# A hybrid diffusion layer on one core: a new order in the recurrence's turns, six heads' queries ahead of the experts, scores amid the second tile's rows, and twelve buffers for the last rows

## The reference, cut to what matters

```
# recurrent mixer, per channel block of 128 (16 of them), two directions d
u  = dwconv(x_l, conv_w, conv_b, left=2)
r  = sigmoid(u @ wa[d] + ba[d]);  i = sigmoid(u @ wx[d] + bx[d])
log_a = -8 * r * softplus(-lam[d]);  a = exp(log_a)
h  = scan(a, sqrt(1 - a*a) * (i * u))          # over time; latents start from the context's state
lru = (h_forward + h_backward) * gelu(g_l)
y  = sigmoid(gates) * (att @ w_o_attn), ... + lru @ w_o_lru + sc @ w_o_sc;  x = x + m2 * (y @ w_out)

# experts: 8 heads, 16 experts a head out of 128 x 128, per token
q = h @ w_q;  s1, s2 = q[0] @ k1, q[1] @ k2;  top 16 of each, top 16 of their sums -> idx, gate
act = gelu(sum_d u_table[idx] * h);  out = sum_k (gate * act)_k * v_table[idx_k]
```

## Time and profile before

| | |
|---|---|
| median of 3 runs | 3000.03 us (2997.91 to 3001.17) |
| profiled execution | 2998.28 us |
| span of its instructions | 2996.7 us |
| mean granted TensorE clock | 0.96 of full speed |
| TensorE / VectorE / ScalarE / POOL busy | 2616.7 / 1958.1 / 970.1 / 612.6 us |
| moved by DMA | 902.91 MB |

### The profile page before, as it was taken

One profiled execution on the slowest core, in us unless ns is written; L12 is line 12 of the kernel. 1 busy time (PEld: TensorE's weight loads), 2 busy tenths in 40 slices (PEclk: granted clock), 3 DMA queues, 4 the chain that ended last, 5 costly groups with the idle time before them and its releaser, 6 DMA issues.

```text
span 2996.7 us, 31604 instructions
## 1 busy us (share of the span) xinstructions
PE 2616.7 (87%) x11037; PEld 1788.6 (60%) x11037; DVE 1958.1 (65%) x2665; ACT 970.1 (32%) x1324; POOL 612.6 (20%) x580
## 2 busy tenths in 40 slices
PE   7999997999989999999999877869697877768777
PEld 3588775888767889998887734333343333323332
DVE  4689996444665878887555775656555655666656
ACT  5567774443454443333444211101011111111100
POOL 0000000000000000000000474334353434443333
PEclk9999998999999999999999998989899898989999
DMA  8733333542324978887565899999999999999998
GB/s 344 274 106 125 112 112 141 196 170 99 141 85 163 367 291 341 343 328 284 202 235 217 344 419 409 421 411 422 421 413 421 403 421 411 421 414 421 421 422 363
DMA packets 126513, 902.91 MB, mean 301 GB/s; under 512 B 14016, under 2 KB 15552, under 8 KB 17216
## 3 DMA queue, kind: packets, MB, share of 16 engines
q0 software_dynamic: 82944, 604.02, 48.9%
q1 hardware_dynamic: 38736, 278.94, 24.8%
q10 hardware_dynamic: 4720, 18.57, 1.6%
HBM read 899.33 MB, written 2.13 MB: 301 GB/s over the span
## 4 chain that ended last, share of the span: by engine, by line
PE 41%; DMA 32%; DVE 13%; issue 10%; ACT 3%; POOL 1%; DVEq 0%; POOLq 0%; ACTq 0%; SPq 0%
DMA u<-in_peer_u,idx 28%; PE ps L462 10%; PE ps L505 8%; PE ps L507 7%; PE ps L506 7%; PE ps L866 4%; DVE u L1882 2%; DVE wl L1295 2%; DMA v<-in_peer_v,idx 2%; DMA w<-in_stream 1%; PE ps L519 1%; ACT wh L962 1%; PE ps L477 1%; DVE ub L1431 1%; POOL v L1980 1%
## 5 line engine op out<-in xcount | busy, mean ns | idle before, releaser
L866 PE MATMUL ps<-v,dg 128*128 128x512 f32 x1920 | 877.0, 613 | 167.0 <-DMA v<-in_peer_v,idx 103.2
L1882 DVE SCALAR_TENSOR_TENSOR u<-u,hN 128x2048 f32<-128x2048 f32 x256 | 586.6, 2292 | 465.8 <-DMA u<-in_peer_u,idx 454.1
L1295 DVE TENSOR_TENSOR wl<-w,wh 128x1024 fp32r<-128x1024 f32 x432 | 524.6, 1222 | 389.7 <-ACT wh L962 389.3
L866 PEld LDWEIGHTS ps<-v,dg 128*128 128x128 f32 x1920 | 367.4, 196 | 672.4 <-issue 497.0
L962 ACT ACTIVATE wh<-w 128x1024 fp32r<-128x1024 f32 x432 | 453.5, 1058 | 590.0 <-PE ps L507 399.4
L1970 POOL DMA_INDIRECT u<-in_peer_u,idx x256 | 280.6, 1096 | 826.5 <-DVE u L1882 437.7
L462 PE MATMUL ps<-both,wh 128*128 128x256 f32 x2048 | 370.9, 284 | 0.3
L1243 ACT ACTIVATE dg<-con,wt 128x128 f32<-128x128 f32 x240 | 93.4, 400 | 841.0 <-PE ps L866 832.5
L1980 POOL DMA_INDIRECT v<-in_peer_v,idx x256 | 297.8, 1163 | 174.3 <-PE ps L866 87.1
L462 PEld LDWEIGHTS ps<-both,wh 128*128 128x128 f32 x2048 | 319.8, 192 | 4.8 <-issue 3.5
L1959 POOL DMA_DIRECT2D mr<-in_wmod x64 | 34.0, 532 | 1357.0 <-DVE br_lo L1688 946.5
(11 more groups left out here) (265 smaller groups left out, 2891.1 us busy)
## 6 DMA issues: line engine op xcount, KB each, us to landing
w<-in_stream SPq DMA_DIRECT2D x260, 1024.0 KB, 4.8
mr<-in_wmod POOLq DMA_DIRECT2D x64, 1024.0 KB, 6.9
wg<-in_gates ACTq DMA_DIRECT2D x8, 512.0 KB, 3.4
wx<-in_stream SPq DMA_DIRECT2D x4, 1024.0 KB, 8.0
u<-in_peer_u,idx POOLq DMA_INDIRECT x256
v<-in_peer_v,idx POOLq DMA_INDIRECT x256, 17.9
xs<-in_ctx ACTq DMA_DIRECT2D x1, 2048.0 KB, 8.0
xs<-in_x ACTq DMA_DIRECT2D x1, 2048.0 KB, 14.8
```

Source lines behind the costliest of these rows:

```text
L866: last = mm(ps[:, b, :], dg[:, k % 4, :], V[n % NV][:, b * 512:(b + 1) * 512], start=(k == 0), stop=(k == TOPK - 1))
L1295: tt(wl[p % SPLITS][:, :, :], W[s][:, q * PIECE:(q + 1) * PIECE, :], wh[p % SPLITS][:, :, :].bitcast(F32), ALU.subtract)\
L1882: stt(U[n % NU][:, :], U[n % NU][:, :], 1.0, hN[:, t, :], ALU.mult, ALU.mult, accum_out=dot[:, t, k:k + 1])\
```

## The change

- **Recurrence.** `rc` goes from VectorE to ScalarE (a Copy with scale and bias behind the square root). ScalarE's `gate_work` is cut in two (`gates`, `powers`); piece 11 is split between them, pieces 12 and 13 before the gelu's sigmoid. VectorE's order becomes `driven`, `gelu_inner`, `low` 11, `decays`, `low` 12, `drives`, `low` 13, `scans`, `low` 14, ..., with `low` 17 and 18 behind `scans(1)`.
- **Last turn.** TensorE does the eight `hx` pieces of OUT0's first turn there: four between the two gate products, four behind them; their splits and lows are put amid the turn's work. OUT0's first turn is taken out of its loop and begins with pieces 8 to 11 already split.
- **Queries.** Heads 4 and 5 are made before `experts(0, 0)` as well. Head 5's weights (2 MB) are loaded by ScalarE's queue at the beginning of `WO0` into the room of `acc`, ahead of that queue's load of `x2`; head 6's follow head 4's in `W`. Queries use banks 4 and 7 by turns. `acc` is no longer cleared in `WO0`: tile 0's first sum is a copy, and tile 1's half is cleared ahead of `dots(1, 0)`.
- **Scores.** `scores(h + 2)` stand behind the ninth row of `experts(h, 1)`.
- **Last rows.** The last 16 rows go into twelve buffers, first the four of U (each once its last dot product is done), then the eight of V, then the first four of V again.

```diff
+        WA = [sb(f"wa{s}", R_HX + 16384 + 8192 * NU + s * HB, [P, HK, CW]) for s in range(2)]
+        def query_bank(h):
+            return h if h < 4 else (4, 7)[h % 2]
+        def last_row_at(k):
+            if k < NU:
+                return U[k], (u_in[k], PH * (2 * TOPK // NU * 16) + 16)
+            i = k - NU
+            return V[i % NV], (v_in[i % NV], (PH - 1) * (2 * TOPK // NV * 16) + TOPK // NV * 16 + 16 * (i // NV + 1))
@@ SyncE @@
-            for h in range(4, PH):
+            for h, of in ((4, 0), (6, 4), (7, 6)):
                 for s in (0, 1):
-                    sp.wait_ge(piece_used, 2 * (WQ0 + 2 * (h - 1 if h > 4 else 0) + s + 1))
+                    sp.wait_ge(piece_used, 2 * (WQ0 + 2 * of + s + 1))
@@ TensorE, last turn of the recurrence, and OUT0 @@
                 gate_products(0)
+                pe.wait_ge(*AD.at(j, "pad1"))
                 if more:
-                    pe.wait_ge(*AD.at(j, "pad1"))
                     proj_both(LRU0, j, 8, 0)
+                else:
+                    wide(OUT0, 0, 16, 0, 0, hx, range(4))
                 gate_products(1)
+                if not more:
+                    wide(OUT0, 0, 16, 0, 0, hx, range(4, 8))
-            out_section(0, OUT0)
+            out_turn(0, OUT0, 0, gated=True)
+            with pe.Fori(1, NW) as j:
+                out_turn(0, OUT0, j)
@@ TensorE, experts @@
+                    last.then_inc(*PE_.inc(f"v{t}{k}"))
+                    if scored is not None and k == TOPK // 2:
+                        scores(scored)
             scores(1)
             route(3)
+            route(4)
+            route(5)
             for h in range(PH):
                 experts(h, 0)
-                if h + 4 < PH:
+                if 6 <= h + 4 < PH:
                     route(h + 4)
-                if h + 2 < PH:
-                    scores(h + 2)
                 if h + 1 < PH:
-                    experts(h, 1)
+                    experts(h, 1, h + 2 if h + 2 < PH else None)
@@ ScalarE @@
+                    act.wait_ge(*AL.at(j, f"e1_{b}"))
+                    fn(aa[:, :, :], aa[:, :, :], ACT.Copy, scale=0.5, bias=0.5).then_inc(*AL.inc(f"rc{b}"))
...
+                gates(0)
                 split(LRU0, j, 8, 11)
-                gate_work(0)
+                powers(0)
+                split(LRU0, j, 8, 12)
+                split(LRU0, j, 8, 13)
                 if more:
-                    for p in (12, 13, 14):
-                        split(LRU0, j, 8, p)
+                    gelu()
+                    split(LRU0, j, 8, 14)
                     pads(j + 1, j * 8 + (2 * LRU0 + 12))
                     split(LRU0, j, 8, 15)
-                gate_work(1)
+                else:
+                    split(LRU0, j, 8, 14)
+                    split(LRU0, j, 8, 15)
+                    gelu()
+                gates(1)
...
+                powers(1)
...
             act.wait_ge(piece_used, 2 * WO0)
+            for s in range(2):
+                act.dma_start(WA[s][:, :, :], a_stream[WQ0 + 10 + s].rearrange("p (k n) -> p k n", n=CW)).then_inc(wa_in[s], 16)
             act.dma_start(x2[:, :, :], a_x.rearrange("(t p) d -> p t d", p=P)).then_inc(x2_in, 16)
@@ VectorE, recurrence @@
-                low(LRU0, j, 8, 11)
                 driven(j, 0)
-                decays(j, 0)
-                gelu_inner(j)
-                drives(j, 0)
                 if more:
+                    gelu_inner(j)
+                    low(LRU0, j, 8, 11)
+                    decays(j, 0)
                     low(LRU0, j, 8, 12)
-                scans(j, 0)
-                if more:
+                    drives(j, 0)
                     low(LRU0, j, 8, 13)
-                lru_out(j, 0)
-                if more:
+                    scans(j, 0)
                     low(LRU0, j, 8, 14)
+                    lru_out(j, 0)
                     taps(j + 1, 0)
-                    low(LRU0, j, 8, 15)
+                else:
+                    low(LRU0, j, 8, 11)
+                    gelu_inner(j)
+                    decays(j, 0)
+                    drives(j, 0)
+                    scans(j, 0)
+                    low(LRU0, j, 8, 12)
+                    lru_out(j, 0)
+                    low(LRU0, j, 8, 13)
+                    low(LRU0, j, 8, 14)
                 driven(j, 1)
                 if more:
+                    low(LRU0, j, 8, 15)
                     taps(j + 1, 1)
                 decays(j, 1)
                 if more:
                     low(LRU0, j, 8, 16)
                 drives(j, 1)
+                if not more:
+                    low(LRU0, j, 8, 15)
+                scans(j, 1)
                 if more:
                     low(LRU0, j, 8, 17)
-                scans(j, 1)
-                low(LRU0, j, 8, 18 if more else 12)
+                    low(LRU0, j, 8, 18)
                 lru_out(j, 1)
@@ VectorE, WO0 and experts @@
-                    nc.vector.memset(acc[:, :, :], 0.0).then_inc(*VF.inc("acc0"))
+            nc.vector.memset(acc[:, 1, :], 0.0).then_inc(*VF.inc("acc0"))
-            dots(1, 0, route(1, 1, 1, False), (0, 0))
+            dots(1, 0, route(1, 1, 1, False), (0, 0, True))
@@ POOL, last tile @@
+            def last_rows(k):
+                row, (landed, _) = last_row_at(k)
+                if k < NU:
+                    pool.wait_ge(*VE.at(PH - 1, f"d1{TOPK - NU + k}"))
+                elif k < NU + NV:
+                    pool.wait_ge(*PE_.at(PH - 1, f"v0{TOPK - NV + k - NU}"))
+                else:
+                    pool.wait_ge(*last_used(k - NV))
```

More of the change, by code:

```diff
@@ L296, in build @@
         wx_in = [sem(f"wx_in{s}") for s in range(4)]
+        wa_in = [sem(f"wa_in{s}") for s in range(2)]
         u_in = [sem(f"u_in{i}") for i in range(NU)]
@@ L994, in lru_turn, with gates @@
             def lru_turn(j, more):
-                def gate_work(b):
+                def gates(b):
                     for d in (0, 1):
@@ L1060, in y_high @@
                         .then_inc(*AY.inc(f"h{b}"))
+            for p in range(8, 12):
+                split(OUT0, 0, 16, p)
             act.wait_ge(*VL.at(NCH - 1, "bl1"))
@@ L1064, in _ @@
             act.dma_start(brow[0:MT, :], a_bmod).then_inc(brow_in, 16)
-            out_section(0, OUT0)
+            out_turn(0, OUT0, 0, ahead=12)
+            with act.Fori(1, NW) as j:
+                out_turn(0, OUT0, j)
             act.wait_ge(crow_in, 16)
@@ L1562, in _ @@
             dve.wait_ge(*VL.at(NCH - 1, "bl1"))
-            with dve.Fori(0, NW) as j:
+            out_turn(0, OUT0, 0, ahead=8)
+            with dve.Fori(1, NW) as j:
                 out_turn(0, OUT0, j)
@@ L1898, in dots, with add @@
                 tt(wt[:, t, :], gw[:, :], gate[:, t, :], ALU.mult).then_inc(*VE.inc(f"w{t}"))
-            def add(h, t):
+            def add(h, t, first=False):
                 dve.wait_ge(*PE_.at(h, f"v{t}{TOPK - 1}"))
-                tt(acc[:, t, :], acc[:, t, :], ps[:, 0:4, :].rearrange("p b n -> p (b n)"), ALU.add).then_inc(*VA.inc(f"ac{t}"))
+                rows = ps[:, 0:4, :].rearrange("p b n -> p (b n)")
+                if first:
+                    nc.vector.tensor_copy(acc[:, t, :], rows).then_inc(*VA.inc(f"ac{t}"))
+                else:
+                    tt(acc[:, t, :], acc[:, t, :], rows, ALU.add).then_inc(*VA.inc(f"ac{t}"))
             def turn(h, odd, used=True):
@@ L1909, in last_row @@
             def last_row(k):
-                j, n = ON_DVE.index(k), TOPK + k
-                dve.wait_ge(v_in[n % NV], (PH - 1) * (2 * TOPK // NV * 16) + 16 * (n // NV + 1))
+                j = ON_DVE.index(k)
+                row, landed = last_row_at(k)
+                dve.wait_ge(*landed)
                 if j:
                     dve.wait_ge(last_dve, j)
-                stt(acc[:, 1, :], V[n % NV][:, :], wt[:, 1, k:k + 1], acc[:, 1, :], ALU.mult, ALU.add).then_inc(last_dve, 1)
+                stt(acc[:, 1, :], row[:, :], wt[:, 1, k:k + 1], acc[:, 1, :], ALU.mult, ALU.add).then_inc(last_dve, 1)
             for _ in route(0, 0, 0, False, True):
@@ L1947, in _ @@
                 dve.wait_ge(last_bank, b + 1)
[L1948 removed]
+                tt(hN[:, 0, cols_], ps[:, 4 + b, :], m5r[:, cols_], ALU.mult).then_inc(*VX.inc(f"x{b}"))
                 dve.wait_ge(*VX.at(0, f"x{b}"))
[L1950 removed]
+                tt(acc[:, 1, cols_], acc[:, 1, cols_], hN[:, 0, cols_], ALU.add).then_inc(*VX.inc(f"o{b}"))
         @block.gpsimd
@@ L1981, in rows_v @@
                                              in_offset=bass.IndirectOffsetOnAxis(ap=idx[:, odd, t, k:k + 1], axis=0)).then_inc(v_in[n % NV], 16)
+            def last_rows(k):
[4 more added lines that the diff above has]
+                    pool.wait_ge(*PE_.at(PH - 1, f"v0{TOPK - NV + k - NU}"))
+                else:
+                    pool.wait_ge(*last_used(k - NV))
+                apart(pool)
+                nc.gpsimd.indirect_dma_start(out=row[:, :], out_offset=None, in_=a_v,
```

(5 more changed lines are left out.)

95 lines of the change are left out of this document (44 added, 51 removed).

## The result

The changed kernel takes 2976.8 us (median of four runs, 2972.49 to 2978.17), the kernel before 2999.09 in the same series (2997.91 to 3001.17). The ratio is 0.9922, with an interval of 0.991 to 0.9934: 22.3 us faster. The forecast was 2967, 32.6 us faster; direction and range hold, and the point is 10 us off. The rest of the document asks where these 10 us are.

A forecast was written before the change was run, and what follows sets the result against it. It took TensorE's path as the bound before 1640 and the DMA queues behind 1670. 6.4 + 8.9 + 0.3 + 5.0 + 12.0 = 32.6 us brings the median of 3000.03 to 2967; range 2959 to 2981.

The forecast's parts named there:

- Loop: Recurrence's looped turns: VectorE loses `rc`, TensorE's 40.2 us becomes the bound; 6.4 us gained, bounds 2 and 7.7.
- The lag of 1.3 us: Recurrence: piece 11, split ahead of the tanh, delays the chain behind TensorE's gate products; 1.3 us subtracted once.
- Last turn: Recurrence's last turn: TensorE reaches `br` 10.3 us earlier, less 1.4 for the lower clock; 8.9 us, bounds 6 and 10.3.
- the third rival: Last turn's pieces: the clock stays at its lower level, 2.8 us more, 2970; chance 0.07.
- WO0 and beginning: WO0: no clearing of `acc`, 0.3 us; experts' beginning: 2 MB fewer on the saturated queue, 5.0 us, lower bound 4.
- Scores: Experts: with the scores moved, no buffer is late and six DMA dips go; 12.0 us, bounds 6 and 12.5.
- Last rows: Experts' end: twelve buffers can't bring the last row in earlier; nothing taken, between -2 and +1 us.
- The thin queue that I named: Last rows: row 3 waits for the last dot product with eight V rows behind it, which may thin the queue.
- The first two rivals: Recurrence's loop keeps its length, 2977, chance 0.14; experts' scores only move their wait to the ninth row, 2979, chance 0.12.
- a wait in the ninth row: Experts, sign that the forecast is wrong: a wait at 852 in a tile's ninth row.
- 17.0: Experts, first U gather to last dot product: forecast gain of 17.0 us, with 5.0 at the beginning and 12.0 for scores.

The follow-up runs named there:

- loop_alone: Kernel before with only the new order in the recurrence's seven looped turns and `rc` on ScalarE; 2993.37 us, ratio 0.9982.
- rc_back: Changed kernel with `rc` on VectorE again; 2980.76 us in one run.
- queries_alone: Kernel before with only the change's lines for the queries, `WA` and `acc`; 2993.67 us, ratio 0.998.
- scores_alone: Kernel before with only the scores moved behind the ninth row of the second tile; 2995.47 us, ratio 0.9984.
- straight kernels: Changed kernel with VectorE's loop over the expert heads written out, in most POOL's too, some with further edits; 2964.97 to 2972.81 us.
- old_last: Changed kernel with the last sixteen rows in V's eight buffers again; 2977.8 us, ratio 0.9928.
- recurrence_alone: Kernel before with all of the change up to OUT0 and nothing of the experts' part; 2984.23 us, ratio 0.9948.
- straight_both: Changed kernel with VectorE's and POOL's loops over the expert heads written out; 2964.97 us, ratio 0.9888.
- straight_scores_back: Changed kernel with both loops over the expert heads written out and the scores in their old place; 2972.81 us, ratio 0.9915.

## Why the prediction was right, and where it was not

- **Loop**, 6.4 forecast: 7.7 by the trace, 5.4 by loop_alone. The size was right and TensorE is the bound, as said. The cause was wrong: the term rested on the 1.37 us that VectorE loses with `rc`, and rc_back keeps `rc` on VectorE and has 6.9 of the 7.7 us. The lag of 1.3 us that I subtracted doesn't show in the sum of the turns.
- **Last turn**, 8.9 forecast. From the end of the scan (445.4) to `br` it takes 35.2 us, 35.7 were forecast; 1.7 us go to the lower clock behind it, 1.4 were taken off. 46.0 - 35.2 - 1.7 = 9.1. Of the third rival this holds: the lower level came back behind two of the three gaps, 3.67 and 2.54 us long, but only one stretch is on the path. The rule of the Trainium skill as the prediction drew it ("TensorE: Matmul & The Clock Gate", Part 1: the default state is throttled, so idle gaps put matmuls at 1.2 GHz) agrees with these two, and taken for every gap it does not agree with the pieces behind 2.01 us, which ran at a granted clock of 1.00.
- **WO0 and beginning**, 0.3 and 5.0. The 10.0 - 5.8 us by tile are 4.2, the lower bound of 4; queries_alone gave 3.0. The first U row came at 1657.0, for which 1655 was forecast; the last query ended near 1727.5, which is the forecast 1742 less the 14.2 us gained by then.
- **Scores**, 12.0: the step that was mis-sized. The mechanism was right: no `scores` among TensorE's waits, POOL's V rows wait for nobody, no wait in a ninth row, and the six dips are gone. The price was wrong. I had turned mean GB/s into time, 20 x (1 - 374/421) and so on. By landed rows the six tiles lose 7.7 us to the scores, and three tiles behind them take 2.6 longer once the scores are gone: 5.1 us net in the changed kernel, 2.3 to 4.7 with straight loops, 1.7 alone. All of these are below my lower bound of 6, though the ratio of scores_alone, 4.8, has an interval that reaches 7.5.
- **What the sum did not have**: VectorE's loop returns. The stall of 5.81 us stood in the trace before, and I had not looked at it. In the changed kernel the two tiles with returns take 3.2 us more than before. scores_alone has 2.9 of these without the second stall, rc_back, without it as well, only 0.3. So what a return costs is clear from the straight kernels in sum alone; why it costs more in the changed kernel than before stays open.
- **Last rows**, 0: right, three times. The thin queue that I named is there (320 GB/s) and costs nothing.
- The first two rivals named nearly the measured time (2977 and 2979), by luck: the loop did not keep its length (40.17 us), and a wait in the ninth row did not come. That the range held is owed to these rivals, to which its upper end had been stretched.

In sum: 6.4 + 8.9 + 0.3 became some 16.5 by the trace (18.2 less the 1.7 given back), within what the dense middle differs by from one profile to the next, and 17.0 became 6.2.

## What to carry to other kernels

A dip in the mean DMA rate is not yet lost time: count when rows land, tile by tile, at the engine that waits for them. Where an engine feeds the queue by what it sets free, look for its idle time that nothing in the trace ends, above all at the return of a loop; with that loop written out the experts took 7.6 us less, more than the change's whole part in the experts (6.2). And a busy time that falls short of the turn says that there are stalls: a new order can fill them without taking work off the engine. Before a difference of 2 us is explained, look at two kernels that share the code of the stage: here such pairs differ by as much.

## What the runs showed of the hardware

The return of VectorE's loop took 5.4 to 5.8 us beside a full DMA queue, in every kernel that has it. A second stall of 2.5 to 2.8 us, between a dot product and the read of its own sum, came with it in the changed kernel, old_last and recurrence_alone, and not in before, rc_back, loop_alone, scores_alone and queries_alone; the loop is the same in all of them, the program ahead of it is not, and why it comes stays open: in the kernel before, too, q14 moves a packet behind that dot product (2227 to 2229), and VectorE does not stand there. POOL's return took 4.7 us in the changed kernel. Written out straight, POOL has more waits of its own (in straight_both 44.0 us for U rows against 29.0, none over 3.0), which cost nothing that "rows" shows.

In all kernels the end came 42 to 43 us behind the last dot product, whatever the mean rate. In the 20 us before that dot product and the 20 us behind it straight_both shows 397 and 360 GB/s, straight_scores_back 422 and 421. What the DMA engines have done ahead in the one case and not in the other the trace does not tell, since it gives only the mean over sixteen engines; this stays open. So does why a row lands about 1 us late once in a tile of 80.5 us; that each such row in the last three tiles follows a packet of the instruction queue is all that the traces show.
